# Linear attention by halving levels on TensorE, and the convolution moved into the projection

## The reference

```python
hn = rms_norm_2(x, mix_norm_g)
gq, gk, gv, glr, gog, cu, dq, dk, dv = split(hn @ w_in)
# linear attention: 4 heads, 32 key channels, 64 value channels
log_a = log_sigmoid(glr @ w_gate + b_gate) / 16
S_t = diag(exp(log_a_t)) S_{t-1} + k_t v_t^T ;  o_t = q_t S_t
o_gla = rms_norm_2(o, norm_g) * silu(gog)
# convolution: 256 channels, 31 taps, causal
z = a * sigmoid(g) ;  y = depthwise_conv(z) + b ; group norm, swish
# differential attention: 4 heads with two query/key pairs of width 64
qh, kh = rms_norm_2(q, qn_g), rms_norm_2(k, kn_g)
p = softmax(causal(qh kh^T / 8)) ;  out = (p1 - lambda p2) v, norm
x = x + concat(o_gla, o_conv, o_diff) @ w_out
```

## Time and profile before

| | |
|---|---|
| median of 3 runs | 3592.49 us (3592.43 to 3595.68) |
| profiled execution | 3596.08 us, its span 3594.2 |
| mean granted clock of TensorE | 0.905 |
| busy: TensorE, VectorE, ScalarE, GpSimd | 86%, 50%, 34%, 33% of the span |
| projection of the second block | 2754.5 to 2999.9 us |
| between projection and units | to 3058.3 us |
| units | to 3184.1 us |
| to the output projection | to 3219.2 us |
| output projection, router, experts | to 3594.2 us |

### The profile page before, as it was taken

How to read it: one execution, slowest core, us unless ns; L and a number is a source line. 1 busy time by engine, 2 the same in 40 slices (tenths; PEclk the granted TensorE clock), 3 DMA queues, 4 the chain that set the end, 5 groups by cost and what they waited for, 6 DMA issues and landing times.

```text
span 3594.2 us, 39189 instructions
## 1 busy us (share of the span) xinstructions
PE 3100.4 (86%) x13486; PEld 2441.9 (68%) x13486; DVE 1786.0 (50%) x2879; ACT 1214.3 (34%) x1827; POOL 1194.4 (33%) x607
## 2 busy tenths in 40 slices
PE   6999898878799997999798878799995795756997
PEld 5887587556588785887587656588783684544665
DVE  4431435577444204441445667544205698764665
ACT  2331324544333214331323544243214212212554
POOL 3444223312244442444223312244441220921222
PEclk9999889998899998999889999899997786567999
DMA  3332222103133321332212103223321551003896
GB/s 120 99 102 97 86 70 71 36 27 103 59 97 96 107 86 53 99 100 97 93 62 77 32 24 100 70 93 94 105 87 33 135 141 30 1 12 134 298 349 225
DMA packets 121883, 341.35 MB, mean 95 GB/s; under 512 B 13472, under 2 KB 49696, under 8 KB 119200
## 3 DMA queue, kind: packets, MB, share of 16 engines
q1 hardware_dynamic: 112336, 322.47, 28.1%
q0 software_dynamic: 6624, 8.41, 0.7%
q10 hardware_dynamic: 2800, 8.91, 0.6%
HBM read 330.30 MB, written 25.17 MB: 99 GB/s over the span
## 4 chain that ended last, share of the span: by engine, by line
PE 76%; DVE 15%; ACT 3%; issue 2%; DMA 1%; POOL 1%; DVEq 0%; ACTq 0%; SPq 0%; POOLq 0%
PE ps L388 19%; PE ps L389 18%; PE ps L391 18%; PE ps L423 4%; PE ps L1548 2%; PE ps L1416 2%; PE ps L1534 1%; PE ps L1535 1%; PE ps L1536 1%; PE ps L654 1%; PE ps L465 1%; DVE xlo L604 1%; DVE rs L1812 1%; PE ps L620 1%; PE ps L749 1%
## 5 line engine op out<-in xcount | busy, mean ns | idle before, releaser
L2162 POOL TENSOR_TENSOR wlo<-raw,whi 128x1024 fp32r<-128x1024 f32 (+1 forms) x368 | 958.0, 2603 | 1901.3 <-ACT whi L480 1901.3
L388 PE MATMUL ps<-xlo,whi 128*128 128x512 f32 x1888 | 780.3, 413 | 127.0 <-DVEq L569 48.8
L389 PE MATMUL ps<-xhi,wlo 128*128 128x512 f32 x1888 | 768.7, 407 | 0.0
L480 ACT ACTIVATE whi<-raw 128x1024 fp32r<-128x1024 f32 (+1 forms) x368 | 409.5, 1113 | 979.8 <-PE ps L391 939.8
L388 PEld LDWEIGHTS ps<-xlo,whi 128*128 128x128 f32 x1888 | 374.6, 198 | 238.9 <-issue 92.8
L391 PE MATMUL ps<-xhi,whi 128*128 128x512 f32 x1888 | 471.0, 392 | 0.0
L389 PEld LDWEIGHTS ps<-xhi,wlo 128*128 128x128 f32 x1888 | 376.2, 199 | 76.3
L391 PEld LDWEIGHTS ps<-xhi,whi 128*128 128x128 f32 x1888 | 358.5, 190 | 75.7
L559 DVE SCALAR_TENSOR_TENSOR xa<-ps,xa 128x512 f32 x56 | 38.7, 692 | 549.2 <-PE ps L391 549.2
L388 PE MATMUL ps<-hlo,whi 128*128 128x512 f32 x704 | 278.9, 396 | 10.0 <-DVE hlo L544 10.0
L389 PE MATMUL ps<-hhi,wlo 128*128 128x512 f32 x704 | 278.3, 395 | 0.0
(11 more groups left out here) (489 smaller groups left out, 5018.4 us busy)
## 6 DMA issues: line engine op xcount, KB each, us to landing
raw<-in_gu SPq DMA_DIRECT2D x176, 512.0 KB, 3.5
raw<-in_mix SPq DMA_DIRECT2D x96, 512.0 KB, 3.6
mraw<-in_w SPq DMA_DIRECT2D x23, 2048.0 KB, 12.0
raw<-in_dn SPq DMA_DIRECT2D x64, 704.0 KB, 4.0
mdraw<-in_w SPq DMA_DIRECT2D x23, 1024.0 KB, 12.6
raw<-in_w SPq DMA_DIRECT2D x32, 512.0 KB, 3.6
vb<-gla_values SPq DMA_DIRECT2D x64, 256.0 KB, 5.7
gate_rows<-tails SPq DMA_DIRECT2D x32, 256.0 KB, 4.2
```

Source lines behind the costliest of these rows:

```text
L388: nc.tensor.matmul(out, whi[:, slot, cols], rlo, start=first and t == 0, stop=False)
L389: nc.tensor.matmul(out, wlo[:, slot, cols], rhi, start=False, stop=False)
L480: nc.scalar.activation(whi[:, s, 0:n], raw[:, r, 0:n], ACT.Copy).then_inc(hi_done, 1)
L2162: nc.gpsimd.tensor_tensor(wlo[:, s, 0:n], raw[:, r, 0:n], whi[:, s, 0:n].bitcast(F32), ALU.subtract).then_inc(w_ready, 1)
```

## The change

The scans go. The 512 tokens form four blocks of 128. The log decay is summed along each block into `dec` (one scan with `resets`). Within a block, the pairs of a query and an earlier key are split by seven levels (64, 32, ..., 1): at a level of n, the keys in the left half and the queries in the right half of each stretch of 2n tokens meet. `halves` holds the keys and queries weighted by the exponential of the distance to the middle, `pe_level` multiplies each head's 32 rows for the four blocks into banks 2 to 5, and `dve_level_copied` takes over the level's pairs into `pairs` with a mask (`copy_predicated`); the diagonal comes from `gk` and `gq` directly. Between blocks, states (`states`, three of 128x256) are carried on. The output is `pairs` times the values plus `q_in` times the state. `gv` is transposed on TensorE and not stored.

The norms: queries get only the gain; their root mean square per token (`rqk`, four matmuls with two columns for each tile, `pe_token_sums`) goes into the scale of the softmax (`dif_scale`). For keys the reciprocal per token is taken on 128x8, widened (`k_wide`), turned by four matmuls (`pe_token_scale`) and multiplied in. All this and the split of `dv` lie under the projection's tiles. The 62 taps of both halves of the convolution run on VectorE, spread over the projection; `pool_conv` goes. The linear attention's part of the mixer's output is split during units 3 and 4. Buffers move, and new semaphore names share numbers with old ones.

```diff
+    LEVELS = (64, 32, 16, 8, 4, 2, 1)
+    T_GATE, T_LEVEL, T_DQ, T_DK, T_DV = 5, 8, 11, 15, 19
...
-            if j == N_GLA - 1:
+            if j == T_GATE - 1:
...
+            if j == T_GATE:
...
-            if j >= N_GLA:
-                ch = j - N_GLA
-                pe.wait_ge(S["qs_ready"], ch + 1)
-                for v in range(4):
+                nc.tensor.matmul(ps[5][:], p2("gateW", rows=16), glr[0:16, :], start=True,
+                                 stop=True).then_inc(S["gate_ps"], 1)
+            if j == T_GATE + 1:
+                pe.wait_ge(S["kv_ready"], 1)
+                pe_level(pe, gk, gq)
+            n = j - T_LEVEL
+            if 0 <= n < len(LEVELS):
+                pe.wait_ge(S["level_ready"], n + 1)
+                pe.wait_ge(S["level_copied"], n + 1)
+                pe_level(pe, halves[n % 3], halves[n % 3])
...
+            t = j - T_DQ - 1
+            if 0 <= t < 4:
+                pe.wait_ge(S["states_ready"], 3)
+                pe_token_sums(pe, t, ps[6][:, 256 + 8 * t:264 + 8 * t])
+            if j == T_DK + 1:
+                pe.wait_ge(S["level_copied"], len(LEVELS) + 1)
+                pe.wait_ge(S["states_ready"], 3)
+                pe.wait_ge(S["q_std"], 1)
+                for qt in range(QT):
+                    out = ps[6 + qt // 2][:, (qt % 2) * 256:(qt % 2) * 256 + 256]
+                    if qt:
+                        nc.tensor.matmul(out, q_in[:, qt, :], states[:, qt - 1, :, :].rearrange("p h v -> p (h v)"),
+                                         start=True, stop=False)
+                    for h in range(4):
+                        ins = nc.tensor.matmul(out[:, 64 * h:64 * h + 64], pairs[:, h, qt, :],
+                                               vT[:, qt, 64 * h:64 * h + 64], start=qt == 0,
+                                               stop=qt == 0 or h == 3)
+                ins.then_inc(S["o_ps"], 1)
+            t = j - T_DK - 1
+            if 0 <= t < 4:
+                if t >= 2:
+                    pe.wait_ge(S["k_std"], t - 1)
+                pe_token_sums(pe, 4 + t, ps[4 + t % 2][:, 8 * t:8 * t + 8])
+            if j == T_DV:
+                pe.wait_ge(S["gl_ready"], 1)
+                for ft in range(2):
...
+                        ins = nc.tensor.transpose(ps[6 + ft][:, qt * P:(qt + 1) * P], o_gla[:, qt, ft * P:(ft + 1) * P],
+                                                  ident)
+                    ins.then_inc(S["aux_ready"], 1)
+            t = j - T_DK - 3
+            if 0 <= t < 4:
+                pe_token_scale(pe, t)
+            if j >= T_DV + 2:
+                pe_dv(pe, j - T_DV - 2)
+        pe_dv(pe, 2)
+        pe_dv(pe, 3)
...
+    def pe_level(pe, left, right):
+        for qt in range(QT):
+            cols = slice(qt * P, qt * P + P)
+            for h in range(4):
+                rows = slice(32 * h, 32 * h + 32)
+                ins = nc.tensor.matmul(ps[2 + h][:, cols], left[rows, cols], right[rows, cols], start=True, stop=True)
+        ins.then_inc(S["level_ps"], 1)
+    def pe_token_sums(pe, t, out):
+        pe.wait_ge(S["sq_ready"], t + 1)
+        for kt in range(QT):
+            ins = nc.tensor.matmul(out[:, 2 * kt:2 * kt + 2], sg[:, t % 2, kt * P:(kt + 1) * P],
+                                   c("blk64")[:, 0:128:64], start=True, stop=True)
+        ins.then_inc(S["stat_used"], 1)
+    def pe_token_scale(pe, t):
+        pe.wait_ge(S["k_r"], t + 1)
+        if t >= 2:
+            pe.wait_ge(S["k_normed"], t - 1)
+        for kt in range(QT):
+            ins = nc.tensor.matmul(ps[2 + t % 2][:, kt * P:(kt + 1) * P], k_wide[:, t % 2, kt * P:(kt + 1) * P], ident,
+                                   start=True, stop=True)
+        ins.then_inc(S["k_r_ps"], 1)
+    def pe_dv(pe, h):
+        pe.wait_ge(S["tile_free"], 2 + T_DV + h + 1)
+        if h == 0:
+            pe.wait_ge(S["og_done"], 2)
+            pe.wait_ge(S["k_std"], 4)
+        for kt in range(QT):
+            ins = nc.tensor.transpose(ps[4 + h][:, kt * P:(kt + 1) * P], dv[:, h, kt * P:(kt + 1) * P], ident)
+        ins.then_inc(S["dv_ps"], 1)
...
+            if j == T_DK + 1:
+                act.wait_ge(S["stat_used"], 4)
+                nc.scalar.activation(rqk[:, 0:32], ps[6][:, 256:288], ACT.Sqrt, bias=eps_ap(RMS_EPS)
+                                     ).then_inc(S["q_std"], 1)
+            t = j - T_DQ
+            if 0 <= t < 8:
+                if t >= 2:
+                    act.wait_ge(S["stat_used"], t - 1)
+                nc.scalar.activation(sg[:, t % 2, :], ps[j % 2][:], ACT.Square).then_inc(S["sq_ready"], 1)
+            nc.scalar.activation(to, ps[j % 2][:], ACT.Copy, scale=scale).then_inc(S["tile_free"], 1)
...
+            if j == T_GATE + 1:
+                for n in range(3):
+                    act_level(act, n)
+                act.wait_ge(S["b_ready"], 1)
+                nc.scalar.activation(q_in[:].rearrange("p q t -> p (q t)"), dec[:], ACT.Exp, scale=1.0 / GLA_TAU
...
+            if j == TILE["cg1"]:
+                act.wait_ge(S["tile_free"], 2 + TILE["cg1"] + 1)
+                nc.scalar.activation(og_sig[:], og[:], ACT.Sigmoid).then_inc(S["z_sig"], 1)
+                nc.scalar.activation(cacc[:], cacc[:], ACT.Sigmoid).then_inc(S["z_sig"], 1)
+            if T_LEVEL + 1 <= j < T_LEVEL + 5:
+                act_level(act, j - T_LEVEL + 2)
...
+    def act_level(act, n):
+        left, right = split_at(halves[n % 3][:], LEVELS[n])
+        act.wait_ge(S["apart"], n + 1)
+        nc.scalar.activation(left, left, ACT.Exp, scale=-1.0 / GLA_TAU)
+        nc.scalar.activation(right, right, ACT.Exp, scale=1.0 / GLA_TAU).then_inc(S["level_exp"], 1)
...
-        for ch in range(N_CHUNK):
-            s = ch % 2
-            dve.wait_ge(S[f"vb_in{s}"], 64 * (ch // 2 + 1))
-            own.link(nc.vector.tensor_tensor(vb[:, s, :, :], vb[:, s, :, :],
-                                            gk[:].unsqueeze(1).broadcast_to([P, 4, T]), ALU.mult))
-            own.wait()
-            if ch >= 2:
-                dve.wait_ge(S["qs_used"], ch - 1)
-            for v in range(4):
-                ins = nc.vector.tensor_tensor_scan(st[:, s, v, :], dec[:], vb[:, s, v, :], 0.0, ALU.mult, ALU.add)
-                if v < 3:
-                    own.link(ins)
+        own.link(nc.vector.tensor_tensor(sg[:, 1, :], sg[:, 1, :], sg[:, 0, :], ALU.subtract))
...
+        taps = iter([(k, u) for u in range(CONV_W) for k in range(2)])
...
+        def tap(count):
+            for k, u in itertools.islice(taps, count):
+                z, w = zp[:, k, u:u + T], p2("convw", CONV_W * k + u)
+                own.wait(own.n - 1 if u else None)
...
+        TAPS = {4: 9, 5: 9, 6: 9, 7: 9}
+        for n in range(len(LEVELS) + 1):
+            dve_level_copied(dve, own, n)
+            m = n + 2
+            if n >= 1 and m < len(LEVELS):
+                dve_apart(dve, m)
+            if n == 2:
+                dve.wait_ge(S["kl_ps"], 1)
+                nc.vector.tensor_copy(k_rows[:].rearrange("p q t -> p (q t)"), ps[6][:, 0:3 * P]).then_inc(S["kl_rows"], 1)
+            if n == 3:
+                dve.wait_ge(S["z_sig"], 1)
+                nc.vector.tensor_tensor(og[:], og[:], og_sig[:], ALU.mult).then_inc(S["vsc"], 1)
+                dve.wait_ge(S["z_sig"], 2)
+                own.link(nc.vector.tensor_tensor(zp[:, :, CONV_W - 1:], zp[:, :, CONV_W - 1:], cacc[:], ALU.mult))
+                dve_states(dve, own)
+            if n >= 4:
+                tap(TAPS[n])
+            if n >= 1 and m < len(LEVELS):
+                dve_weighted(dve, m)
+        for t in range(4):
+            dve_hi_lo(dve, own, t)
+            tap(2)
+        dve.wait_ge(S["o_ps"], 1)
...
+        for t in range(4):
+            dve.wait_ge(S["k_std"], t + 1)
+            r = rqk[:, 32 + 8 * t:40 + 8 * t]
+            own.link(nc.vector.reciprocal(r, r))
             own.wait()
...
+        def gla_parts(u):
+            if u in (3, 4):
+                split_mix(dve, own, u - 3, gla_t[:, u - 3, :])
...
+    def dve_apart(dve, n):
+        if n >= 3:
+            dve.wait_ge(S["level_ps"], n - 1)
+        c2 = 2 * LEVELS[n]
+        b = dec[:].rearrange("p (b c) -> p b c", c=c2)
+        nc.vector.tensor_tensor(halves[n % 3][:].rearrange("p (b c) -> p b c", c=c2), b,
+                                b[:, :, c2 // 2 - 1:c2 // 2].broadcast_to([P, T // c2, c2]), ALU.subtract
+                                ).then_inc(S["apart"], 1)
+    def dve_weighted(dve, n):
+        dve.wait_ge(S["level_exp"], n + 1)
+        left, right = split_at(halves[n % 3][:], LEVELS[n])
+        nc.vector.tensor_tensor(left, left, split_at(gk[:], LEVELS[n])[0], ALU.mult)
+        nc.vector.tensor_tensor(right, right, split_at(gq[:], LEVELS[n])[1], ALU.mult).then_inc(S["level_ready"], 1)
+    def dve_level_copied(dve, own, n):
+        mask = (ident if n == 0 else level_mask[n - 1][:]).bitcast(mybir.dt.uint32)
+        dve.wait_ge(S["level_ps"], n + 1)
```

(53 more changed lines are left out.)

341 lines of the change are left out of this document (181 added, 160 removed).

## The result

The changed kernel takes 3471.3 us, the median of four runs (3462.6, 3470.0, 3472.7, and one of 6651.0 that something else disturbed and that the ratio leaves out), against 3592.5 before. The ratio is 0.965, 95% interval 0.9632 to 0.9668: faster, by about 121 us of 3592.5 (119 to 132 by the interval), where 96 were forecast. The profiled execution took 3470.0 us, its span is 3468.2.

The account below looks back on a forecast made before the run. TensorE and VectorE were both full in the projection's chunks, with other limits elsewhere. From 3596.1 us, 89 less before the units and 7 within them gave 3500, 3496 as a median; range 3468 to 3532.

Parts of the forecast that it names:

- Tiles 8 to 14 each carry a level: Projection's level tiles on TensorE: old measured cycle of 10.8 us each kept, 75.6, plus 4.8 of small work.
- TensorE up to tile 7: Projection from first tile's end: tiles at 5.44 us, value transposes 2.0, gate matmul 1.1, first level 3.5; 44.7 us.
- Tiles 15 to 22: Projection's last eight tiles on TensorE: 6.4 us each, 51.2, plus 17.8 of other small work.
- Tail and waits: Projection's end: 3 us for waits between level engines, 5.5 for last copies, subtractions and the engines' meeting.
- VectorE's sum: Projection from the gate matmul: 118 us of operations plus 28 lost to GpSimd's weight splits, 146 without waits.
- ScalarE's order matters at tile 10: Projection: two wide sigmoids and table loads stand ahead of level 4's exponentials; otherwise order matters only at the gates.
- Units: The 32 attention units: 7 us less, from taps and GpSimd delays gone before group ends; bounds 3 and 13.
- Behind them: The stretch after the attention units was to keep its 35.1 us.
- The first: Projection: levels overlap or keep the clock up, TensorE gets lighter, VectorE is the bound; 3468 to 3482; chance 0.17.
- rival 2: Tiles 8 to 22: clock stays low, 3552; partly so, or with dear predicated copies, 3515 to 3550; chance 0.18 for both.
- rival 3: Slower than before: VectorE's 32 predicated copies cost from 3.7 us each and eat all 96 us; chance 0.03.
- rival 4: No change: queues merely trade waits, the new projection filling the old one's 292 us; chance 0.01.

## Why the prediction was wrong

**The step that failed** is "Tiles 8 to 14 each carry a level: I take the measured cycle of 10.8 us as it is, clock included, 75.6". With the small work it gave 80.4 us; 63.8 were measured, 16.6 of the 23.5 us by which the stretch was over-priced. The cycle held two things that did not carry over: 3.5 us for 16 matmuls of 128 rows that follow one another, where these overlap and take 1.17; and a tile of 7.3 us for 5.44, at a clock that had been low behind 4-column products, where it now stays at 0.94 on the mean. The experiments show both. In seven tiles the first is 16.3 us less and the second up to 13.0. Against them stand TensorE's waits, 8.6 of the 63.8 us, where the forecast had 3 for all its tiles; the remaining 4 us, clock lost behind these waits among them, were not taken apart.

**TensorE up to tile 7**: right but for the first level, 41.6 against 44.7. **Tiles 15 to 22** at 6.4 us: 69.2 against 69.0, though by two errors that cancel: 6.4 us of wait for `k_wide` in place of a lower clock in every tile. **Tail and waits**: 8.5 against 4.5.

**VectorE's sum**: 146 forecast from the gate on, 127 measured (the windows above). The predicated copies cost 0.726 us (0.70 assumed); the taps' least and median are 0.73 and 0.74; about 22 us went to operations that met GpSimd's subtraction, 28 forecast. The rest of the difference, by subtraction, is small operations priced too high. That ScalarE's order matters at tile 10 came true: 7.4 us of wait there, and 7.9 us of the stretch when it was changed.

**Units**: 8.0 us against 7, and group ends as in the earlier trace rows: 20.5 us for three, down from 26.3. **Behind them**: 36.4, kept but for 1.3 us.

**Rivals.** The first is what came, nearly: it had the units begin 182 to 189 us behind the end of tile 0, measured 179, and 3468 to 3482, measured 3471. Its condition, levels that overlap, is shown. Its other half, VectorE as the bound, is not: 49 us of its work left out gave 10.6. The estimate from the Trainium skill ("TensorE: Matmul & The Clock Gate", Part 3: packing small matmuls), 3.07 times, was 1.1 us a level where the row gave 3.5, and the trace agrees with it: 1.17. No neighbouring matmuls of before used different row groups, so no row spoke for the overlap; but none spoke against it either, and 0.17 took that silence for evidence. The low clock (rival 2) did not come, except behind waits of TensorE and in the units, 0.53. The lowest window stands behind a wait of 2.25 us:

```profile
2841.00:2847.00 6.00, 4.96 (x43) 4.58 (x44) 5.96 (x8) 1.72 (x4) 2.72 (x1) 0.59 0.00 0
```

What rival 2 took from the units, that small products with few rows leave the clock low, did not carry over: from 2811 to 2841, with three levels of 32 rows, it is 1.00. No run tells what transposes do to it.

A dear predicated copy (rival 3) and no change (rival 4) are refuted by 0.726 us and by the time.

## What to carry to other kernels

A measured cycle carries over only if what fills it does: take it apart into matmul time, shape and clock before using it for other matmuls, and give an overlap that no row excludes its full weight. When two engines are both near full, look not only at their sums but at which single operation is late. An exponential taken ahead of two sigmoids brought 7.9 us of the stretch and GpSimd's subtraction in two parts 7.1, with no work left out, where leaving out nearly all taps brought 10.6; moving half of the taps away brought as much as leaving out 60 of 62. A wait of TensorE that is removed pays more than its length where the clock had fallen behind it.

## What the runs showed of the hardware

- 16 fp32 matmuls of 32 rows and 128 columns take 1.17 us when neighbours lie in different row groups (and banks), 2.82 when four in a row share one, both at full clock. With 128 rows a change of bank alone gives no overlap.
- TensorE busy for 80.4 of 82 us had a granted clock of 0.75 with 16 products of 4 columns in each cycle, and 1.00 with 16 of 128 columns. Fewer columns made them no cheaper: 3.63 to 5.54 us for the 16 thin ones, 3.73 to 3.81 for the wide.
- A tap on VectorE (two SBUF inputs, 0.74 us) that meets GpSimd's subtraction takes up to 2.88 us where that is one instruction of 1024 columns, and 1.76 where it is two of 512. A cast with one input (0.42 us) took up to 2.38. None of the 32 predicated copies out of PSUM was longer than 0.75 us, though 17 of them met it.
